# Scan ticks reordered, r operands built beside the substitution, in a two-layer decoder kernel on one Trainium2 core

## The chip, the cores and the metric

The kernel runs on one NeuronCore of a Trainium2 chip. The metric is the device time of one execution in microseconds (us), the median of several. The engines are TensorE (PE), VectorE (DVE), ScalarE (ACT), GpSimd (Pool) and SyncE (SP), which here only issues DMAs. Each has its own instruction stream, and they meet at semaphores.

## The reference

A decoder trunk of two layers, 512 tokens of width 1024, all in float32. Layer 0 is an RWKV-7 time mix (16 heads of 64) and a mixture of experts (32 experts); layer 1 is sparse attention and another mixture of experts. The change lies in the time mix:

```
r, k, v = xr @ w_r, xk @ w_k, xv @ w_v
kk = normalised(k * k_k);  k = k * (1 + (a - 1) * k_a)
step:  sa    = state @ (-kk_t)
       state = state * w_t + sa (kk_t * a_t)^T + v_t k_t^T
       y_t   = state @ r_t
y = group_norm(y) + sum(r * k * r_k) * v        # the second term is the bonus
out = (y * g) @ w_o
```

## The kernel before

**Layout.** Activations are kept transposed: eight tiles `m` of 128 channels (two heads) by 512 tokens, in regions of SBUF: `r_T`, `a_T` (from kk), `b_T` (kk * a), `k_T`, `v_T`, `g_T`, `l_T` (running log decay). The recurrence is done in chunks of 64 tokens, 8 chunks by 8 tiles = 64 packs (`PACKS`), numbered `n = 8 c + m`.

**Projections.** Weights come in tiles of 512 KB through a ring of four slots (`wring`, one region): 8 tiles each for k, v, r, and later w_o. SP loads them in the order of its program, each after the matmuls on the slot's earlier tile (`proj_mm`).

**First operands.** While PE projects v, DVE runs `k_scale(m)` (L940, L944, L945), then multiplies `a_T` by the decay (L962) and its first columns by -1 (L964, 8 elements a row), ACT makes the factor and the exponentials (L644 to L651), and Pool multiplies `b_T` (L481). PE weaves into its v matmuls, in quarters of a tile ("parts"), the product `k_inverse(m)` and, two turns later, `gram_of(m)`; DVE masks the result into `gram` (L954). SP stores the gram tiles to DRAM (L318) and, when all have landed, reads them back in another shape as `solve` (L349).

**Substitution.** The 32x32 triangular blocks are inverted column by column on DVE, steps i = 2 to 31: a product over i*i*2 elements (L976) and a reduction (L979), each waiting for the other. PE projects r beside it and ACT copies the first five r tiles out (L633). When the substitution is done SP stores the result (L354), and reads it back into `gram` with eight DMAs, four for each half of the packs (L360).

**r operands.** ACT waits for `inverse_out`. Then for each m it makes `exp(-l)` and `exp(l)` (L666, L667); DVE multiplies r * rk * k (L987) and r by the decay (L990); Pool multiplies k by the growth (L485); PE sums the first product over each head (`bonus_mm`), DVE multiplies that with v into `l_T` (`bonus_out`, L950).

**Scan.** 64 packs go through a pipeline of PE stages, one tick apart. In tick t PE runs, in this order, `rh(t-1)`, `u(t-2)`, `w(t-3)`, `u2(t-4)`, `y` and `s` of `t-5`, and last the transposes (L1569) and `p_late` products of pack t. Every stage has one PSUM bank and is copied out by ACT (`p_tr` L709, `p_rh` L678, w L685, y L702) or DVE (`p_late` L1028 and L1030, u L1004, u2 L1010, state L1018). `rh(n)` needs the copies of `p_tr` and `p_late` of pack n. Pool expands the operands of pack t+1 (L473, four products) and then, in the same tick, `x_e(t)` (L510), which needs the inverse. ACT's and DVE's orders follow PE's.

After the scan come the group norm, the w_o projection, and the rest of the network, which takes three quarters of the time.

Of the kernel before, what the change touches and what calls it, by code (L numbers as in the profile page):

```python
# [10 lines left out]
P = 128  # L11
# [3 lines left out]
NK = D // P  # L15
# [62 lines left out]
} | {f"bias_h{i}": (f"wring{i}", 128) for i in range(4)}  # L78
# [8 lines left out]
def decoder_program(nc, d, out):  # L87
    stack = ExitStack()
    with stack:
# [59 lines left out]
        tmp = region(2).rearrange("p (x s t) -> p x s t", x=4, s=2)  # L149

# [6 lines left out]
        solve = region(2)[:, 0:2048].rearrange("p (b s t) -> p b s t", b=2, s=32)  # L157
        ones_at = region(2)[:, 0:2048].rearrange("p (b n) -> p b n", b=2)[:, :, 0:1024:33]
# [129 lines left out]
        SOLVED = 1 + 2 * 30  # L288
        block = stack.enter_context(nc.Block())
# [3 lines left out]
        def _(sp):  # L293
# [16 lines left out]
            def load_ring(q, rows):  # L310
                sp.dma_start(wring[:, q % 4, :], rows).then_inc(sem(f"wring{q % 4}"), 16)
# [9 lines left out]
            for q in range(8):  # L321
# [7 lines left out]
                load_ring(q, wk_rows[q, :, :])  # L329
            for m in range(4):  # L330
                sp.wait_ge(sem("mix_used"), 24 + m + 5)
                load_ring(8 + m, d["a_wv"][m, :, :])
            sp.wait_ge(sem("mix_ready"), 48)
            sp.dma_start(head_of, d["head_of"].rearrange("h (m n) -> h m n", m=NP)).then_inc(sem("bias_in"), 16)
            for m in range(4, NP):
                sp.wait_ge(sem("proj_mm"), 8 + m - 3)
                load_ring(8 + m, d["a_wv"][m, :, :])
# [26 lines left out]
            for m in range(4):  # L364
                sp.wait_ge(sem("proj_mm"), 21 + m)
                load_ring(24 + m, wo_rows[m, :, :])
            sp.wait_ge(sem("pe_s"), PACKS)
            sp.wait_ge(sem("ev_s"), PACKS)
            for m in range(4, NP):
                sp.wait_ge(sem("wo_used"), m - 3)  # L370
                load_ring(24 + m, wo_rows[m, :, :])
# [94 lines left out]
        def _(pool):  # L466
# [1499 lines left out]
```

## Time and profile before

| | us |
|---|---|
| median of 3 runs (2197.18 to 2200.33) | 2199.89 |
| the profiled execution: time, span | 2202.11, 2200.1 |
| PE busy | 1958.9 (89%) |
| DVE, ACT, Pool busy | 705.7, 433.7, 190.6 |
| tiles for k to the start of the substitution | to 233.4 |
| substitution | 233.4 to 302.9 |
| first transposes of the scan | 330.3 |
| last tick with transposes ends | 578.3 |
| mean granted TensorE clock (share of full speed) | 0.954 |

Times within the profile are from the span's start. "Idle before" is the time an engine stood ahead of an instruction, with what released it. Granted clock is 1.00 at full speed (2.4 GHz) and 0.50 at half (1.2 GHz). PEld is the loading of weights into the array, which overlaps matmuls. A matmul of 512 float32 columns shows as two records of 0.43 us.

### The profile page before, as it was taken

Reading aid. Unit: us, or ns where it says so; the run is one execution under the profiler, and the core shown is the slowest. Engines: PE = TensorE matmul, PEld = TensorE weight load, DVE = VectorE, ACT = ScalarE, POOL = GpSimd, SP = SyncE. Lnnn points to the kernel's source line nnn. Section 1 sums busy time; section 2 is a strip of 40 time slices with the busy share of each in tenths; the row PEclk is TensorE's granted clock in tenths of the full one; section 3 lists DMA queues with packets and bytes.
Section 4 is the critical chain, followed back from the end, with each engine's and each line's share of the span. In section 5 each row is a group of like instructions: output and inputs, shape, how many; then the busy total and the mean of one; then the engine's idle time right before and its main releaser. Section 6 shows DMA issues by size and latency. Waiting matters only on the chain.

```text
span 2200.1 us, 27449 instructions
## 1 busy us (share of the span) xinstructions
PE 1958.9 (89%) x10860; PEld 1085.4 (49%) x10860; DVE 705.7 (32%) x1545; ACT 433.7 (20%) x1094; POOL 190.6 (9%) x377
## 2 busy tenths in 40 slices
PE   6999958888887999999997799999888999999993
PEld 2344417777636444444442347866546444444441
DVE  4307783444483311111110431465413111111113
ACT  2313013444401000000000201266410000000001
POOL 0002024444200000000000100011100000000001
PEclk9999977999997999999999799999997999999996
DMA  9272220000036799999995821100225999999994
GB/s 271 40 158 52 92 77 1 2 2 1 1 128 260 296 415 426 427 429 431 423 430 203 290 71 35 77 30 30 102 107 213 387 428 426 429 429 423 429 427 146
DMA packets 71750, 497.47 MB, mean 226 GB/s; under 512 B 25796, under 2 KB 30404, under 8 KB 54470
## 3 DMA queue, kind: packets, MB, share of 16 engines
q1 hardware_dynamic: 56982, 465.20, 52.0%
q10 hardware_dynamic: 12336, 22.09, 4.1%
q0 software_dynamic: 2304, 8.39, 1.1%
q8 instruction: 90, 1.47, 0.3%
q14 instruction: 38, 0.31, 0.0%
HBM read 460.46 MB, written 34.14 MB: 225 GB/s over the span
## 4 chain that ended last, share of the span: by engine, by line
PE 81%; DVE 11%; ACT 3%; issue 3%; DMA 2%; POOL 1%; ACTq 0%; SPq 0%; DVEq 0%; POOLq 0%
PE bank L1372 76%; DVE arena L976 2%; PE bank L1838 2%; ACT arena L709 1%; DVE arena L1175 1%; DVE arena L979 1%; PE bank L1569 1%; PE bank L1638 1%; DVE arena L1332 1%; PE bank L1380 1%; DMA arena<-y_rows,ints 1%; DVE arena L964 0%; DVE arena L1211 0%; DVE arena L987 0%; DMA arena<-gram 0%
## 5 line engine op out<-in xcount | busy, mean ns | idle before, releaser
L1372 PE MATMUL bank<-arena 128*64 128x512 f32 (+11 forms) x9336 | 1742.9, 425 | 66.8 <-DVE arena L1175 44.4
L1372 PEld LDWEIGHTS bank<-arena 128*128 128x128 f32 (+5 forms) x9336 | 913.6, 165 | 832.0 <-issue 724.4
L736 ACT ACTIVATE arena<-bank 128x512 f32<-128x512 f32 x64 | 38.2, 597 | 821.9 <-PE bank L1372 821.9
L1113 DVE TENSOR_TENSOR arena<-bank,vec 128x512 f32<-128x512 f32 x64 | 44.3, 692 | 346.7 <-PE bank L1372 346.7
L1167 DVE TENSOR_TENSOR arena<-arena,bank 128x256 f32<-128x256 f32 x64 | 27.0, 421 | 339.0 <-ACT arena L732 339.0
L527 POOL DMA_INDIRECT arena<-y_rows,ints x16 | 17.5, 1091 | 1233.2 <-DMA y_rows<-arena 1228.9
L473 POOL TENSOR_TENSOR arena<-arena,const 128x128 f32<-128x128 f32 x256 | 97.4, 413 | 124.3 <-PE bank L1372 123.0
L1372 PE MATMUL bank<-state,arena 128*128 128x128 f32 (+1 forms) x256 | 52.8, 337 | 42.1 <-ACT arena L709 40.2
L1372 PE MATMUL bank<-arena,const 128*128 128x512 f32 (+5 forms) x96 | 44.8, 615 | 36.8 <-DVE arena L987 21.1
L839 ACT ACTIVATE arena<-arena,small 128x128 f32<-128x128 f32 (+3 forms) x128 | 70.4, 552 | 25.2 <-DVE small L1332 25.1
L1175 DVE COPY arena<-bank 128x256 f32<-128x256 f32 x64 | 26.9, 420 | 144.6 <-PE bank L1638 144.6
L1372 PEld LDWEIGHTS bank<-state,arena 128*128 128x128 f32 x256 | 41.7, 233 | 53.4 <-ACT arena L709 51.1
L1332 DVE CUSTOM_DVE_ANT_0 arena<-bank,arena 128x128 f32<-128x128 f32 (+3 forms) x128 | 57.4, 486 | 30.9 <-PE bank L1372 30.9
L1838 PE MATMUL bank<-const,arena 128*128 128x128 f32 x320 | 48.5, 282 | 10.4 <-DVE arena L1343 10.4
L1838 PEld LDWEIGHTS bank<-const,arena 128*128 128x128 f32 x320 | 33.8, 141 | 39.1 <-issue 26.3
L551 ACT ACTIVATE arena<-arena 128x1024 f32<-128x1024 f32 x20 | 21.1, 1054 | 154.6 <-DVE arena L1061 60.5
L1372 PEld LDWEIGHTS bank<-arena,const 128*128 128x128 f32 (+1 forms) x96 | 17.5, 236 | 62.5 <-issue 28.1
L732 ACT ACTIVATE arena<-bank 128x256 f32<-128x256 f32 x64 | 24.6, 384 | 120.4 <-issue 80.4
L709 ACT ACTIVATE arena<-bank 128x384 f32<-128x384 f32 x64 | 31.4, 491 | 71.5 <-PE bank L1372 71.5
L1380 PE MATMUL bank<-const,arena 128*128 128x128 f32 x96 | 21.4, 396 | 25.4 <-DVE arena L864 25.3
L976 DVE TENSOR_TENSOR arena<-arena 128x8 f32<-128x8 f32 (+29 forms) x30 | 41.0, 1366 | 1.0
L1004 DVE COPY arena<-bank 128x128 f32<-128x128 f32 x64 | 18.7, 292 | 68.7 <-PE bank L1372 68.7
(206 smaller groups left out, 1099.3 us busy)
## 6 DMA issues: line engine op xcount, KB each, us to landing
arena<-m_w SPq DMA_DIRECT2D x64, 4096.0 KB, 21.6
arena<-m_w SPq DMA_DIRECT2D x64, 2048.0 KB, 13.5
y_rows<-arena ACTq DMA_DIRECT2D x128, 128.0 KB, 9.6
y_rows<-arena SPq DMA_DIRECT2D x2, 3840.0 KB, 41.0
arena<-kv_w SPq DMA_DIRECT2D x3, 2048.0 KB, 12.7
rev_bias<-arena ACTq DMA_DIRECT2D x1, 5120.0 KB, 56.0
arena<-a_wk SPq DMA_DIRECT2D x8, 512.0 KB, 15.6
arena<-a_wv SPq DMA_DIRECT2D x8, 512.0 KB, 3.9
```

The costliest lines, as they stand in the source:

```text
L473: nc_op = nc.gpsimd.tensor_tensor(dst.rearrange("p (a t) -> p a t", a=2), spread(src[:, m, c * C:c * C + C], 1, 2), mask, ALU.mult)
L709: nc.scalar.activation(bkv_s[:, n % 8, :], p_tr, ACT.Copy).then_inc(sem("ev_tr"), 1)
L736: nc.scalar.activation(yb[:, n % 2, :], bank[6 + n % 2][:, :], ACT.Copy).then_inc(sem("yb_ready"), 1)
L839: last = nc.scalar.activation(probs[:, n % 3, a, 0:P * (j + 1)], probs[:, n % 3, a, 0:P * (j + 1)], ACT.Exp, scale=-1.0, bias=low[:, n % 3 ...
L976: nc.vector.tensor_tensor(terms, solve[:, :, 0:i, 0:i], spread(solve[:, :, 0:i, i], 2, i), ALU.mult).then_inc(sem("solved"), 1)
L1113: nc.vector.tensor_tensor(xgT[:, p % 2, 4 * q:4 * q + 4, :], bank[2 + q][:, :].rearrange("p (k t) -> p k t", k=4), spread(v8(f"m_ln{l}")[: ...
L1167: nc.vector.tensor_tensor(gated[:, n % 2, :], silu_h[:, n % 2, :], bank[4 + n % 2][:, 256:512], ALU.mult).then_inc(sem("gated_ready"), 1)
L1175: nc.vector.tensor_copy(hT[:, n % 2, :, :, :], bank[n % 2][:, 0:256].rearrange("p (i q t) -> p i q t", i=2, q=2)).then_inc(sem("h_ready"), 1)
L1332: last = nc.vector.tensor_tensor_reduce(out=probs[:, n % 3, a, 0:P * (j + 1)], in0=bank[2 * (n % 2) + a][:, 0:P * (j + 1)], in1=bias_h[:, ...
L1372: return nc.tensor.matmul(dst, lhsT, rhs, start=start, stop=stop)
L1380: last = nc.tensor.transpose(bank[k][:, P * j:P * j + P], xn[:, j, P * k:P * k + P], ident)
L1838: last = nc.tensor.transpose(bank[4 + a][:, P * s:P * s + P], probs[:, n % 3, a, P * s:P * s + P], ident)
```

## The change

1. In the scan, PE, ACT and DVE take the transposes and their copies first in each tick, and `rh` with its copy last.
2. ACT and Pool build the r operands. ACT writes the exponentials to `r_dec` and `r_grow` (one buffer each), and copies each r tile out twice, once scaled by rk (`r_k`). Pool makes three products for each m: `r_k * k`, `r * decay`, `k * growth`. They wait for `b_ready` and `a_ready`, not for `inverse_out`. PE makes `bonus(m-1)` after r tile m. DVE takes the first five `bonus_out` between substitution steps, after steps 24, 25, 27, 29 and 30, and the rest behind.
3. `solve` moves from region 2 to slots 2 and 3 of the weight ring. v tiles 4 to 7 and all r tiles go through slots 0 and 1. v6 is loaded after store_gram(4), v7 after store_gram(7) and v5's matmuls; all r tiles after `solve`. w_o tiles wait for all r tiles.
4. The first columns of `a_T` (L964) are negated by ACT (`a_first`), which gram_of waits for.

```diff
-        solve = region(2)[:, 0:2048].rearrange("p (b s t) -> p b s t", b=2, s=32)
+        solve = region(4)[:, 2048:4096].rearrange("p (b s t) -> p b s t", b=2, s=32)
+        r_dec, r_grow = region(2)[:, 0:512], region(2)[:, 512:1024]
+        r_k = region(2)[:, 1024:2048].rearrange("p (s t) -> p s t", s=2)
+        BONUS_AT = (24, 25, 27, 29, 30)
...
# SP
-            for m in range(4, NP):
+            for m in (4, 5):
                 sp.wait_ge(sem("proj_mm"), 8 + m - 3)
-                load_ring(8 + m, d["a_wv"][m, :, :])
-            for m in range(4):
+                load_ring(m % 2, d["a_wv"][m, :, :])
+            for m in range(5):
                 store_gram(m)
             sp.wait_ge(sem("proj_mm"), 13)
-            load_ring(16, d["a_wr"][0, :, :])
-            for m in range(4, NP):
+            load_ring(0, d["a_wv"][6, :, :])
+            for m in range(5, NP):
                 store_gram(m)
             sp.wait_ge(sem("proj_mm"), 14)
-            load_ring(17, d["a_wr"][1, :, :])
+            load_ring(1, d["a_wv"][7, :, :])
             sp.wait_ge(sem("gram_out"), 32 * 16)
...
-            for m in range(2, NP):
-                sp.wait_ge(sem("proj_mm"), 13 + m)
-                load_ring(16 + m, d["a_wr"][m, :, :])
+            for m in range(NP):
+                sp.wait_ge(sem("proj_mm"), 15 + m)
+                load_ring(m % 2, d["a_wr"][m, :, :])
...
# Pool
+            pool.wait_ge(sem("a_ready"), NP)
             for m in range(NP):
                 pool.wait_ge(sem("decays"), m + 1)
+                pool.wait_ge(sem("proj_ev"), 17 + m)
+                nc.gpsimd.tensor_tensor(r_k[:, m % 2, :], r_k[:, m % 2, :], k_T[:, m, :], ALU.mult).then_inc(sem("rk_ready"), 1)
                 pool.wait_ge(sem("rk_ready"), m + 1)
-                nc.gpsimd.tensor_tensor(k_T[:, m, :], k_T[:, m, :], tmp[:, 2, m % 2, :],
-                                        ALU.mult).then_inc(sem("operands_pool"), 1)
+                nc.gpsimd.tensor_tensor(r_T[:, m, :], r_T[:, m, :], r_dec, ALU.mult).then_inc(sem("r_scaled"), 1)
+                nc.gpsimd.tensor_tensor(k_T[:, m, :], k_T[:, m, :], r_grow, ALU.mult).then_inc(sem("operands_pool"), 1)
...
# ACT
                 act.wait_ge(sem("proj_mm"), 16 + m + 1)
+                if m >= 2:
+                    act.wait_ge(sem("bonus_mm"), m - 1)
+                nc.scalar.activation(r_k[:, m % 2, :], bank[1 + (m + 2) % 3][:, :], ACT.Copy, scale=v8("rk")[:, m:m + 1])
...
+                act.wait_ge(sem("k_scaled"), m + 1)
+                nc.scalar.activation(a_T[:, m, 0::C], a_T[:, m, 0::C], ACT.Copy, scale=-1.0).then_inc(sem("a_first"), 1)
...
-            for m in range(5):
+            act.wait_ge(sem("b_ready"), NP)
+            for m in range(NP):
+                if m:
+                    act.wait_ge(sem("operands_pool"), m)
+                nc.scalar.activation(r_dec, l_T[:, m, :], ACT.Exp, scale=-DECAY)
+                nc.scalar.activation(r_grow, l_T[:, m, :], ACT.Exp, scale=DECAY).then_inc(sem("decays"), 1)
                 r_out(m)
-            act.wait_ge(sem("inverse_out"), 16)
...
# DVE
-                                               ALU.mult, ALU.mult)
-                nc.vector.tensor_scalar(kk_v[:, :, 0:1], kk_v[:, :, 0:1], -1.0, None, ALU.mult).then_inc(sem("a_ready"), 1)
+                                               ALU.mult, ALU.mult).then_inc(sem("a_ready"), 1)
...
                 nc.vector.tensor_reduce(solve[:, :, 0:i, i], terms, axis=AX.X, op=ALU.add).then_inc(sem("solved"), 1)
+                if i in BONUS_AT:
+                    bonus_out(BONUS_AT.index(i))
...
# PE
+            def bonus(m):
+                pe.wait_ge(sem("rk_ready"), m + 1)
+                if m == 0:
+                    pe.wait_ge(sem("gram_ev"), NP)
+                if m >= 2:
+                    pe.wait_ge(sem("bonus_ev"), m - 1)
+                mm(bank[6 + m % 2][:, :], head_ones, r_k[:, m % 2, :]).then_inc(sem("bonus_mm"), 1)
...
                 last.then_inc(sem("proj_mm"), 1)
+                if m:
+                    bonus(m - 1)
+            bonus(NP - 1)
...
# PE, ACT and DVE: in every tick the block of the transposes (n = tick) stands first;
# on PE and ACT the block of rh (n = tick - 1) stands last
             for tick in range(PACKS + 6):
-                n = tick - 1
-                if 0 <= n < PACKS:
+                n = tick
+                if n < PACKS:
```

## Rows read from the trace of the kernel before

**Rows 1.** Busy time by stage: window, length, engines' busy time, granted clock, DMA share, GB/s.
```profile
336.00:359.00 23.00, 19.85 (x116) 17.29 (x117) 5.95 (x23) 7.23 (x23) 9.80 (x27) 0.61 0.00 1
359.00:579.00 220.00, 184.21 (x1768) 162.91 (x1766) 89.97 (x342) 104.16 (x342) 105.57 (x279) 1.00 0.01 2
```

**Rows 2.** Chain of work in order of time: start, us, what.
```profile
336.01 1.62 PE bank L1372 x6
...
358.69 2.46 PE bank L1372 x24
...
569.80 0.33 PE bank L1569 x3
570.13 0.46 PE bank L1372 x4
570.61 0.50 ACT arena L709
...
578.93 2.93 PE bank L1372 x34
```

**Rows 3.** Timeline of one tick, PE and ACT: start, us, instruction, idle before.
```profile
571.20 0.46 PE L1372 MATMUL bank<-state,arena 128*128 128x128 f32 x2 [0.63 <-ACT arena L709]
...
571.92 0.28 ACT L678 ACTIVATE arena<-bank 128x128 f32<-128x128 f32 x1 [0.82 <-PE bank L1372]
```

**Rows 4.** Timeline around the substitution, SP's queue and DVE.
```profile
224.83 0.34 SPq L349 DMA_DIRECT2D arena<-gram  x1
...
233.40 0.11 DVE L972 MEMSET arena<- 128x64 f32 x1 [13.52 <-DMA arena<-gram]
...
302.92 0.33 SPq L354 DMA_DIRECT2D inverse<-arena  x1
306.81 5.24 SPq L360 DMA_DIRECT2D arena<-inverse  x8
```

**Rows 5.** Timeline of the first operands, DVE and Pool.
```profile
184.48 0.69 DVE L962 SCALAR_TENSOR_TENSOR arena<-arena 128x504 f32<-128x504 f32 x1
184.52 1.77 POOL L481 TENSOR_TENSOR arena<-arena 128x512 f32<-128x512 f32 x1 [172.50 <-DVE arena L945]
185.08 1.24 DVE L964 TENSOR_SCALAR arena<-arena 128x8 f32<-128x8 f32 x1
```

**Rows 6.** Timeline of the v projection's end: weight loads, PE, ACT.
```profile
203.16 0.29 PEld L1372 LDWEIGHTS bank<-arena 16*128 16x128 f32 x2 [0.76 <-issue]
...
207.22 0.29 PEld L1372 LDWEIGHTS bank<-arena 16*128 16x128 f32 x2 [0.76 <-issue]
...
218.00 1.15 PE L1372 MATMUL bank<-arena 64*64 64x64 f32 x32 [1.53 <-DVE arena L954]
...
229.68 0.60 ACT L629 ACTIVATE arena<-bank 128x512 f32<-128x512 f32 x1 [6.27 <-PE bank L1372]
```

**Rows 7.** Groups of instructions: count, busy us, mean ns, idle before.
```profile
L473 POOL TENSOR_TENSOR arena<-arena,const 128x128 f32<-128x128 f32 x256 | 97.4, 413 | 124.3 <-PE bank L1372 123.0 <-DVE arena L950 1.2
L543 POOL TENSOR_TENSOR arena<-arena 128x512 f32<-128x512 f32 x16 | 20.3, 1270 | 233.3 <-DVE arena L1359 233.3
...
L987 DVE SCALAR_TENSOR_TENSOR arena<-arena,vec 128x512 f32<-128x512 f32 x8 | 9.3, 1168 | 5.2 <-ACT arena L667 5.2
...
L950 DVE TENSOR_TENSOR arena<-bank,arena 128x512 f32<-128x512 f32 x8 | 5.5, 684 | 0.8 <-PE bank L1372 0.8
```

**Rows 8.** Timeline of the substitution: two of its 30 reductions (i = 16, 24).
```profile
246.90 0.69 DVE L979 TENSOR_REDUCE arena<-arena 128x32 f32<-128x512 f32 x1
...
268.30 1.35 DVE L979 TENSOR_REDUCE arena<-arena 128x48 f32<-128x1152 f32 x1
```

**Rows 9.** The clock: two windows (as rows 1) and PE's first work after a pause.
```profile
296.00:298.00 2.00, 0.00 (x0) 0.00 (x0) 1.97 (x2) 0.00 (x0) 0.00 (x0) 0.50 0.00 0
...
614.14 2.90 PE L1372 MATMUL bank<-arena 128*128 128x512 f32 x3 [6.39 <-issue]
...
620.00:622.00 2.00, 2.00 (x6) 0.80 (x5) 2.00 (x1) 0.00 (x0) 0.00 (x0) 0.94 0.00 0
```

More of the change, by code:

```diff
@@ L77 @@
     "cmp_w1_in0": ("router_in", 32),
-} | {f"bias_h{i}": (f"wring{i}", 128) for i in range(4)}
+} | {f"bias_h{i}": (f"wring{i}", n) for i, n in enumerate((176, 176, 80, 80))}
 def spread(ap, axis, n):
@@ L702, in _ @@
                     nc.scalar.activation(y_T[:, n % NP, (n // NP) * C:(n // NP) * C + C], p_y, ACT.Copy).then_inc(sem("ev_y"), 1)
-                n = tick
-                if n < PACKS:
-                    act.wait_ge(sem("pe_tr"), n + 1)
-                    if n >= 8:
-                        act.wait_ge(sem("pe_s"), n - 7)
-                        act.wait_ge(sem("ev_tr"), n - 7)
-                    nc.scalar.activation(bkv_s[:, n % 8, :], p_tr, ACT.Copy).then_inc(sem("ev_tr"), 1)
+                n = tick - 1
+                if 0 <= n < PACKS:
+                    act.wait_ge(sem("pe_rh"), n + 1)
+                    if n >= 2:
+                        act.wait_ge(sem("pe_u"), n - 1)
+                        act.wait_ge(sem("ev_rh"), n - 1)
+                    nc.scalar.activation(rhs_s[:, n % 2, :], p_rh, ACT.Copy).then_inc(sem("ev_rh"), 1)
             for m in range(NP):
@@ L1460, in gram_of @@
                 pe.wait_ge(sem("a_ready"), m + 1)
+                pe.wait_ge(sem("a_first"), m + 1)
                 pe.wait_ge(sem("b_ready"), m + 1)
@@ L1507, in _ @@
             for tick in range(PACKS + 6):
-                n = tick - 1
-                if 0 <= n < PACKS:
+                n = tick
+                if n < PACKS:
                     m, c = n % NP, n // NP
-                    pe.wait_ge(sem("ev_tr"), n + 1)
-                    pe.wait_ge(sem("ev_late"), n + 1)
-                    if c:
-                        pe.wait_ge(sem("ev_s"), n - NP + 1)
-                    else:
-                        pe.wait_ge(sem("state_zero"), 1)
-                    if n:
-                        pe.wait_ge(sem("ev_rh"), n)
-                    mm(p_rh, a_e[:, n % 4, :], state[:, m, :], True, False)
-                    mm(p_rh, ak_t[:, n % 4, :], bkv_s[:, n % 8, 256:384], False, True).then_inc(sem("pe_rh"), 1)
+                    pe.wait_ge(sem("ex_late"), n + 1)
+                    if n:
+                        pe.wait_ge(sem("ev_tr"), n)
+                        pe.wait_ge(sem("ev_late"), n)
+                    e = bkv_e[:, n % 2, :]
+                    cs = slice(c * C, c * C + C)
+                    for i in range(3):
+                        nc.tensor.transpose(p_tr[:, P * i:P * i + P], e[:, P * i:P * i + P], ident)
+                    mm(p_late[:, 0:64], e[:, 0:128], r_T[:, m, cs])
+                    mm(p_late[:, 64:192].rearrange("p (w t) -> p w t", w=2), e[:, 128:256],
+                       ra_T[:, :, m, cs]).then_inc(sem("pe_tr"), 1)
                 n = tick - 2
@@ L1558, in _ @@
                     mm(p_s, s8[:, 128:256], s8[:, 256:384], False, True).then_inc(sem("pe_s"), 1)
-                n = tick
-                if n < PACKS:
+                n = tick - 1
+                if 0 <= n < PACKS:
                     m, c = n % NP, n // NP
-                    pe.wait_ge(sem("ex_late"), n + 1)
-                    if n:
-                        pe.wait_ge(sem("ev_tr"), n)
-                        pe.wait_ge(sem("ev_late"), n)
-                    e = bkv_e[:, n % 2, :]
-                    cs = slice(c * C, c * C + C)
-                    for i in range(3):
-                        nc.tensor.transpose(p_tr[:, P * i:P * i + P], e[:, P * i:P * i + P], ident)
-                    mm(p_late[:, 0:64], e[:, 0:128], r_T[:, m, cs])
-                    mm(p_late[:, 64:192].rearrange("p (w t) -> p w t", w=2), e[:, 128:256],
-                       ra_T[:, :, m, cs]).then_inc(sem("pe_tr"), 1)
+                    pe.wait_ge(sem("ev_tr"), n + 1)
+                    pe.wait_ge(sem("ev_late"), n + 1)
+                    if c:
+                        pe.wait_ge(sem("ev_s"), n - NP + 1)
+                    else:
+                        pe.wait_ge(sem("state_zero"), 1)
+                    if n:
+                        pe.wait_ge(sem("ev_rh"), n)
+                    mm(p_rh, a_e[:, n % 4, :], state[:, m, :], True, False)
+                    mm(p_rh, ak_t[:, n % 4, :], bkv_s[:, n % 8, 256:384], False, True).then_inc(sem("pe_rh"), 1)
             pe.wait_ge(sem("ev_y"), PACKS)
```

96 lines of the change are left out of this document (35 added, 61 removed).

## The prediction

> **What bounds the kernel now.** I read the stages first. After the scan TensorE is busy almost without a pause to the end; nothing there is edited, and a transfer there waits only on work of that part, so I let it shift as a block. The change lies in operand building, substitution and scan. In the scan one engine should be full, yet PE is busy 184 of 220 us at full clock, after a start at an average of 0.61 [rows 1]. The chain of waits shows why [rows 2]: PE transposes pack n (0.33) and makes its `p_late` products (0.46), then stands until ACT L709 has copied `p_tr`, since `rh(n)` comes next. From 570.57 to 571.20 nothing runs on PE [rows 2, 3]. The tick is 3.864 us ((578.93 - 358.69)/57), of which 0.63 is this stall. DVE, ACT and Pool are busy 90, 104 and 106 of 220 us, under 1.9 a tick [rows 1], so PE's order is the bound.
>
> Ahead of the scan the chain is serial: gram tiles, their way through DRAM, the substitution on DVE (233.40 to 302.9), the inverse stored and read back, and only then exponentials, products, bonus and expansion [rows 4]. Tick 2 begins at 336.01 [rows 2], 33.1 us after the last reduction. Beside the substitution Pool does nothing and ACT next to nothing; PE, with the r tiles, is done before it.
>
> **Part 1: DVE's first column goes to ACT (`a_first`).** DVE L964 touches 8 elements and takes 1.24 us. It ends at 186.32, together with Pool L481 (184.52 + 1.77 = 186.29): it waits for Pool [rows 5]. Without it DVE could go 1.15 us faster in each of 8 turns, but PE then sets the pace: its turn is 4.06 us (203.16 to 207.22), and it had been standing for DVE by the end (1.53 before the gram at 218.00) [rows 6]. After the k_inverse at 207.22 the gram products start at about 208.3; two turns without k_inverse (a part of 1.72, 1.15 of gram, gaps: 3.2) put gram(7) at 214.65 instead of 218.00, so v5 ends at 219.25 instead of 222.6 (229.68 - 6.87 is its copy, 222.81) [rows 6]. The last gram store is then issued by 218.4 and lands by 220.0; the v7 load, which SP now holds until v5 is done, goes at 219.3 to 219.8. The load of `solve` leaves at 220.05, not 224.83 [rows 4]: **-4.8**. On ACT, `a_first(m)` waits for `k_scaled(m)`; v_out(2) and k_factor(m+1) queue behind it. Two exponentials and a factor (2 us) still fit before DVE's second need of them, 3 us on. Nothing charged.
>
> **Part 2: weight slots.** v6 and v7 go through two slots. v6 loads behind store_gram(4), around 210, and lands 5 us later, needed at 219.3. v7 lands about 224, needed at 226. Each r load has one tile of PE (6.87) for a landing of 3.5 to 4.7. Zero; if one is late, PE shifts by that and the slack of part 3 takes it. `solve` in other addresses: zero.
>
> **Part 3: r tiles beside the substitution.** It now starts at 220.05 + (233.40 - 224.83) = 228.6. With its own length, 69.5, and five bonus_outs of 0.68 [rows 7] placed in it (**+3.5**), it ends at 301.6 plus what the new Pool work costs it. That work is 24 products of 128x512, 1.27 each when alone [rows 7]. The before trace has no Pool product beside L976, so nearest rows bound it. When DVE L962 (both inputs in SBUF) had started 0.04 before it, Pool's L481 took 1.77; when Pool was running, L964 and L987 (1.17 on average, about 0.7 for such a shape alone, as L950) stretched to its end or past it [rows 5, 7]. L976 has both inputs in SBUF, so I let each hold the other off, and let reductions pass. A Pool product then falls into the reduction at its turn, and the next L976 starts late by 1.3 less the reduction: 0.69 long at i = 16 when r0 arrives (v6, v7 and r0, 6.87 each, after v5: 239.9), 1.35 at i = 24 [rows 8]. First tile 1.9, second 1.1, third 0.5, and about 0.9 for each of four later tiles, where a second product squeezes into the reduction; the last falls behind the final L976. **+7.0**, between 0 (they pass each other) and 17.5 (A, B and C of each tile run back to back, 3.8 less the reduction).
> The Trainium skill (SBUF — State Buffer, Who interferes with whom) says that an op with two SBUF inputs and a GpSimd op that reads SBUF exclude each other for a whole instruction, and that a reduction never contends. Rows agree for the first half (1.77 against 1.27). By it the sum below holds; without it, it would be 7 lower.
>
> Is the r chain in time? PE: r0 to 239.9, then r1, bonus0, r2, bonus1, r3 (three tiles, two products of 0.86) to 262.2; bonus2 waits for bonus_ev 1, after step 24 (36.25 into the substitution [rows 8], 264.9, and 3.5 of delays), and r4 to r7 queue behind it. Then 6.9 a tile (its copies stand 6.87 apart) plus the waits for steps 27 and 29: r7 ends about 305, ACT's copies 306, three products 310, the last bonus_out 311, expansions 0 and 1 314. The inverse is there at 308.6 + 8.3 = 316.9, so 3 us are left. PE idles 6 us before r4; in the old idle behind r7 (about 291) the clock was at the lower level by 296 [rows 9]. r4 partly at the lower level, 1.2 GHz, costs 3 us, which the waits for steps 27 and 29 take up.
>
> **Part 4: from the last reduction to tick 2.** The eight exponential and product rounds (22 us) are gone from here. What stays: store (3.9), eight inverse loads from +3.9, the first four landed at +8.3 (four issues of 0.65 and 1.9 to land) [rows 4], Pool x_e(0) 0.42, expand(2) 1.52 (four at 0.41, overlapping [rows 7]; before PE's tr(2), since x_e(0) stands ahead of it), so tick 2 at +10.35 instead of +33.1: **-22.7**.
>
> **Part 5: ticks 2 to 7.** They took 22.7 (336.01 to 358.69), at a granted clock of 0.61 on average [rows 1, 2]. In the new order PE has work without the gap from tick 2 on. Another stretch, unbroken from 614.14, had its clock back in 620 to 622 [rows 9]. With 6 us at 1.2 GHz: ticks 2 and 3 take 6.6, tick 4 (no y and s) 2.0, Pool-bound, ticks 5 and 6 3.23 each: 15.0, **-7.7**. If the clock stays low as before, ticks take twice 3.23 and it is -0.7.
>
> **Part 6: 57 full ticks.** The new first stage gives ACT a whole tick for `p_tr`. rh is now last, and u needs its copy: PE end to ACT start 0.26, copy 0.28, plus 0.06 to PE, 0.60 [rows 3], under the 0.79 of transposes and p_late [rows 2]. DVE's s copy and ACT's y copy end before their users too. 57 x 0.635: **-36.2**. At the end, with no tr to cover it, rh's copy shows once: +0.4.
>
> Sum: -4.8 + 3.5 + 7.0 - 22.7 - 7.7 - 36.2 + 0.4 = -60.5. Profiled execution 2202.11 (span 2200.1): 2141.6; it lies 2.2 above the median 2199.89, so **2139.4**; I say 2140.
>
> **Rivals.**
> - *Heavier port waits, or a late clock.* Products back to back add 10.5 (2150); the low clock to tick 7 adds 7 (2146); both 2157. For: ticks 0 and 1 come alone, with a pause before 2, and nothing shows who wins the port when both wait. Against: B waits for A's semaphore, which lets DVE in. 15% for over 2150.
> - *r chain ends last.* If PE stays at 1.2 GHz from r4 on (idle before it, waits at steps 27 and 29), a tile takes 13.7: r4 to r7 and their bonuses run from 269 to 331, the operands are ready at 337 and tick 2 comes at 342 instead of 319: 2163. For: the idle at 291 to 296 lost the clock [rows 9]. Against: r4 alone is unbroken work long enough to bring it back. 8%.
> - *The tick keeps part of its stall*, through rh's copy or expansion: at 3.5 us it adds 15, 2155. ACT is in order and rh's copy is behind y's. 6%.
> - *Slower than before.* The wait of u on rh's copy in each tick, on the path and not under the transposes. Cover is 0.79; a round trip of 1.73 (PE, ACT, PE) costs 64 x 0.94 = 60 us, all that is gained; from there on it decides. At 2.0 the time is 2140 + 64 x 1.21 = 2217. Rows give 0.60 [rows 3], but ACT is in order, and a slow y copy ahead would push it. 3%.
> - *The move buys nothing ahead of the scan*: only parts 5 and 6 remain, 2156. Needs the inverse to have been the bound already; it is not, 33.1 against 10. Inside the 6% above.
> - *Less than 2133*: no port waits at all, 2132. 5%.
>
> Likeliest, with 63%, 2133 to 2150. A difference under 0.2% (4.4 us) is about what a measurement can't tell from none. The range 2132 to 2160 leaves out the late r chain, the slow case and part of the low end, under 2 in 10. Faster 0.95, same 0.02, slower 0.03.
>
> **What would show it.** `solve` load near 220; memset near 228.6; Pool products of 1.3 to 4 us and L976 longer than before, reductions not; last reduction near 308; tick 2 near 319; granted clock 1.0 within 10 us of it; ticks of 3.23 with no PE idle. Wrong if PE waits on ACT L678's copy in each tick, if r7 is later than the inverse, or if the substitution grows by over 20.

## The result and the profile after: 2124.6 us, faster by 3.6%, below the forecast range

The changed kernel takes 2124.58 us (median of 4 runs, 2123.94 to 2126.38) against 2200.11 for the kernel before on the same chip (4 runs, 2197.18 to 2215.65): a ratio of 0.9644, 95% interval 0.9599 to 0.969. The forecast was 2140, range 2132 to 2160. The sign held, and so did the mechanism of the largest part; the gain in the profiled spans is 76.2 us (2200.1 to 2123.9) where 60.5 were forecast.

Busy time by stage in the kernel after (columns as in [rows 1]). The stages are: last reduction to tick 2, tick 2 to the start of tick 7, and the 57 full ticks (7 to 63). A tick starts with its first instruction: `rh` in the old order, the transposes in the new.

```profile
303.10:317.70 14.60, 6.26 (x21) 4.27 (x20) 2.96 (x7) 3.19 (x6) 11.06 (x21) 0.55 0.86 219
317.70:331.00 13.30, 13.30 (x116) 12.36 (x115) 5.45 (x23) 7.23 (x23) 10.78 (x29) 0.85 0.19 77
331.00:502.00 171.00, 171.00 (x1769) 158.87 (x1766) 84.59 (x343) 104.11 (x342) 104.60 (x276) 1.00 0.01 2
```

PE, the first busy column, is busy 171.00 of 171.00 us where it was 184 of 220 [rows 1], for the same 57 ticks.

SP's queue and DVE around the substitution, kernel after (as [rows 4]):

```profile
219.95 0.34 SPq L352 DMA_DIRECT2D arena<-gram  x1
...
225.98 0.11 DVE L978 MEMSET arena<- 128x64 f32 x1 [9.44 <-DMA arena<-gram]
...
303.11 0.33 SPq L357 DMA_DIRECT2D inverse<-arena  x1
307.01 5.22 SPq L363 DMA_DIRECT2D arena<-inverse  x8
```

Two ticks of PE in the kernel after (as [rows 3]; the first two lines are `rh(n-1)`, L1520 the transposes, "x14" is `p_late`, u, w and u2; the lines left out are y and s):

```profile
327.51 0.39 PE L1369 MATMUL bank<-state,arena 128*128 128x128 f32 x2
327.73 0.39 PE L1369 MATMUL bank<-arena 128*128 128x128 f32 x2
327.95 0.49 PE L1520 MATMUL bank<-const,arena 128*128 128x128 f32 x3
328.28 1.08 PE L1369 MATMUL bank<-arena 128*128 128x64 f32 x14
...
330.95 0.49 PE L1520 MATMUL bank<-const,arena 128*128 128x128 f32 x3
```

From transposes to transposes it is 3.00 us, with no idle entry. The times of both spans, split at the same events, against the terms of the forecast:

| stretch | before | after | change | forecast |
|---|---|---|---|---|
| to the substitution's start (memset) | 233.40 | 225.98 | -7.4 | -4.8 |
| substitution, to SP's store | 69.52 | 77.13 | +7.6 | +10.5 |
| store to tick 2 | 33.09 | 14.63 | -18.5 | -22.7 |
| tick 2 to the start of tick 7 | 22.68 | 13.21 | -9.5 | -7.7 |
| 57 full ticks | 220.24 | 171.00 | -49.2 | -36.2 |
| end of the scan | 10.55 | 11.63 | +1.1 | +0.4 |
| the rest of the network | 1610.6 | 1610.3 | -0.3 | 0 |
| sum | | | -76.2 | -60.5 |

The four stretches ahead of the full ticks were off by 2 to 4 us each, of both signs, together -3.1; the full ticks were off by 13.0, five sixths of the error of 15.7.

Where the chain of waits runs ahead of the scan in the kernel after (start, us, what; the first line is the third bonus product, `bonus(2)`, with r4 behind it):

```profile
266.98 9.66 PE bank L1369 x18
...
287.66 2.59 POOL arena L489
290.32 1.27 POOL arena L491
291.60 4.40 POOL arena L492
296.05 0.51 issue
296.56 0.61 ACT arena L675
...
306.99 1.27 POOL arena L489
310.41 0.70 DVE arena L957
```

The chain passes from DVE to PE at step 24 and then goes by Pool's r products and ACT's exponentials, not by the inverse.

### The profile page after: what moved, and what is told of

It is laid out like the page before. It is cut to its first block, busy times and chain, and to the rows that moved or that the text cites. A ratio compares the mean times of both kernels' runs of the same rounds, so it can differ in the third digit from the quotient of the medians.

```text
span 2123.9 us, 27456 instructions
## 1 busy us (share of the span) xinstructions
PE 1932.7 (91%) x10860; PEld 1075.2 (51%) x10860; DVE 682.8 (32%) x1521; ACT 438.3 (21%) x1110; POOL 225.5 (11%) x393
## 4 chain that ended last, share of the span: by engine, by line
PE 85%; DVE 7%; issue 3%; ACT 2%; POOL 2%; DMA 1%; ACTq 0%; DVEq 0%; SPq 0%; POOLq 0%
PE bank L1369 80%; PE bank L1840 2%; DVE arena L1172 1%; DVE arena L982 1%; PE bank L1520 1%; PE bank L1640 1%; DVE arena L1329 1%; PE bank L1377 1%; DVE arena L985 1%; DMA arena<-y_rows,ints 1%; DVE arena L1208 1%; POOL arena L489 0%; POOL arena L492 0%; DVE arena L871 0%; DMA arena<-x 0%
## 5 line engine op out<-in xcount | busy, mean ns | idle before, releaser
L1369 PE MATMUL bank<-arena,const 128*128 128x512 f32 (+5 forms) x96 | 39.9, 562 | 27.7 <-DVE arena L1091 12.2
L1369 PE MATMUL bank<-state,arena 128*128 128x128 f32 (+1 forms) x256 | 47.6, 317 | 1.9 <-DVE arena L894 1.9
L982 DVE TENSOR_TENSOR arena<-arena 128x8 f32<-128x8 f32 (+29 forms) x30 | 46.2, 1540 | 0.9
L549 POOL TENSOR_TENSOR arena<-arena 128x512 f32<-128x512 f32 x16 | 20.3, 1272 | 233.0 <-DVE arena L1356 233.0
```

The costliest lines, as they stand in the source:

```text
L982: nc.vector.tensor_tensor(terms, solve[:, :, 0:i, 0:i], spread(solve[:, :, 0:i, i], 2, i), ALU.mult).then_inc(sem("solved"), 1)
L1369: return nc.tensor.matmul(dst, lhsT, rhs, start=start, stop=stop)
```

## The experiments

Each ran beside the kernel before on its chip. A median is of 4 to 6 runs; where one run was made, it says so. The kernel before spreads more than the gains of some parts: beside experiments 1 to 3 it took 2193.18 to 2230.58 us. So their ratios are wide, and the parts are compared by their profiles, with the profile before. The landing of the solve load is given from SP's issue to DVE's memset: 8.57 us in the profile before, 6.03 in the one after.

**1. Only the new order of the scan.** The kernel before, with the stages of PE, ACT and DVE in the changed kernel's order and nothing else.

```diff
 for tick in range(PACKS + 6):
+    n = tick
+    ...   # transposes, p_late; on ACT and DVE their copies
-    n = tick - 1
-    ...   # rh
     n = tick - 2
...
-    n = tick
-    ...
+    n = tick - 1
+    ...   # PE and ACT: rh
```

> Kernel before with only the new order of the scan's stages on PE, ACT and DVE. Theory A (the stall is worth 0.86 us a tick, because the 0.63 shown is counted from a modelled end that holds the product's drain, and the weight load behind it starts late too): full ticks of 3.00 us, PE without idle time; about 2141 to 2143. Theory B (the stall is worth the 0.63 shown, and the other 0.23 comes from the rebuilt operands or the later clock): ticks of 3.23, about 2155.

Measured 2142.83 (2141.44 to 2145.34), ratio 0.9692 (0.9609 to 0.9775). A tick of its profile:

```profile
453.67 0.43 PE L1372 MATMUL bank<-arena,state 128*128 128x64 f32 x2
...
456.67 0.43 PE L1372 MATMUL bank<-arena,state 128*128 128x64 f32 x2
```

3.00 us again, with no idle between. The stall was worth 0.864 us in each tick, as theory A had it for the size, and the 3.23 of the prediction fell.

**2. Only the operands.** The changed kernel with the scan's stages in the old order (the diff above, reversed).

> Changed kernel with the old order of the scan's stages. Ticks back at 3.86 with 0.63 of idle time each. Additive theory: it keeps what the first operands and the hidden r products gave, 18 us, so about 2182; the low clock at the scan's start stays for some 20 us, as before. Rival (the two parts need each other, the earlier scan only pays with the new order): under 10 us, above 2190.

Measured 2182.99 (2182.45 to 2186.84), ratio 0.9875 (0.979 to 0.9961). The tick is 3.86 again, with the old wait:

```profile
450.41 0.46 PE L1369 MATMUL bank<-state,arena 128*128 128x128 f32 x2 [0.63 <-ACT arena L716]
...
454.27 0.46 PE L1369 MATMUL bank<-state,arena 128*128 128x128 f32 x2 [0.63 <-ACT arena L716]
```

In spans, the order alone gives 60.6 (2200.1 - 2139.5), the operands alone 19.9 (2200.1 - 2180.2), both 76.2: nearly a sum. Each alone also had a solve load that landed sooner than in the profile before (from issue to memset 5.3 and 5.9 instead of 8.6), which the sum counts twice. The low clock left sooner than expected here: it rose at about 330, 12 us after tick 2 began (318.3), and not 20.

**3. Another order without the stall.** The kernel before with y and s moved behind the transposes and `p_late`, rh still first.

```diff
     ...   # u2, tick - 4
-    n = tick - 5
-    ...   # y and s
     n = tick
     ...   # transposes and p_late
+    n = tick - 5
+    ...
```

> Kernel before with the transposes one place earlier than they were (before y and s), rh still first in the tick. Theory A (any order that keeps PE from standing gives the whole 0.86): ticks of 3.00 as in the scan-only run, within 0.05, about 2142. Rival C (the new order packs weight loads better than the old one does, apart from the stall): ticks of 3.2, about 2155. Rival D (ACT's copy of p_tr is not ready behind y and s either): idle time before rh remains, ticks above 3.3.

Measured 2150.2 (2148.75 to 2151.6), ratio 0.9722 (0.9638 to 0.9805). Its ticks take 2.955 us, and they show where the stall's size comes from. The four records of `p_late`, then y and s (128x64 x2 and x8), then rh:

```profile
452.50 0.61 PE L1372 MATMUL bank<-arena 128*128 128x64 f32 x4
452.95 0.33 PE L1372 MATMUL bank<-arena,state 128*128 128x64 f32 x2
453.12 1.11 PE L1372 MATMUL bank<-arena 128*128 128x64 f32 x8
454.06 0.39 PE L1372 MATMUL bank<-state,arena 128*128 128x128 f32 x2
454.29 0.85 PE L1372 MATMUL bank<-arena 128*128 128x128 f32 x12
```

The same four records in the kernel before, ahead of the stall:

```profile
569.96 0.61 PE L1372 MATMUL bank<-arena 128*128 128x64 f32 x4
571.20 0.46 PE L1372 MATMUL bank<-state,arena 128*128 128x128 f32 x2 [0.63 <-ACT arena L709]
571.50 0.85 PE L1372 MATMUL bank<-arena 128*128 128x128 f32 x12
```

The group is shown as 0.61 long in both. With work behind it, the next begins 0.45 after its start; ahead of the wait it is 1.24. That is 0.79, of which 0.63 stands as idle and 0.16 in the shown length of the last product. rh then takes 0.30 to its successor instead of 0.23 (0.22 in other ticks), another 0.07: together 0.86. The last 0.05 of the 0.91 that this order gains comes from how the records follow each other: the first of y is 0.06 ahead of the next instead of 0.16, the first transpose 0.16 instead of 0.11. So a little of rival C is true, 0.05 a tick. Theory A's 2142 was missed; the total is 8 us above the first experiment: its first ticks have no y and s yet to fill the gap and go on with the stall at half clock until about 353, and its solve load landed 3.2 us later.

**4. The changed kernel without the 24 Pool products.** Only a test: they are left out, so `r_T`, `k_T` and the bonus are not scaled; semaphores are raised in their place.

```diff
-                nc.gpsimd.tensor_tensor(r_k[:, m % 2, :], r_k[:, m % 2, :], k_T[:, m, :], ALU.mult).then_inc(sem("rk_ready"), 1)
-                pool.wait_ge(sem("rk_ready"), m + 1)
-                nc.gpsimd.tensor_tensor(r_T[:, m, :], r_T[:, m, :], r_dec, ALU.mult).then_inc(sem("r_scaled"), 1)
-                nc.gpsimd.tensor_tensor(k_T[:, m, :], k_T[:, m, :], r_grow, ALU.mult).then_inc(sem("operands_pool"), 1)
+                pool.sem_inc(sem("rk_ready"), 1)
+                pool.sem_inc(sem("r_scaled"), 1)
+                pool.sem_inc(sem("operands_pool"), 1)
```

> Changed kernel without the 24 products of the r operands on Pool (r_k * k, r * decay and k * growth are left out, their semaphores are still raised). Port theory: the substitution shrinks from 77.1 to about 72.5 (69.5 and five bonus_outs of 0.6), L982 at i = 21 takes 1.7 and not 2.7; tick 2 then hangs on the inverse, 10.4 behind the last reduction; about 2117. Rival (the growth is DVE waiting for PE's bonus products): the substitution stays at 77.

Measured 2114.7 (one run). The substitution takes 72.2 us (memset 224.85, store 297.02) instead of 77.1. Its step i = 21 and the end of its wait for the inverse:

```profile
248.32 1.70 DVE L981 TENSOR_TENSOR arena<-arena 128x882 f32<-128x882 f32 x1
...
304.56 0.41 POOL L515 TENSOR_TENSOR arena<-arena,const 128x128 f32<-128x128 f32 x1 [0.74 <-DMA arena<-inverse]
...
307.28 0.88 PE L1519 MATMUL bank<-const,arena 128*128 128x128 f32 x3
```

Tick 2 at 307.28 is 10.26 after the store: the +10.35 that the prediction gave for the inverse as the bound. So the products cost the substitution 5.0 us (77.13 - 72.17) and the way to tick 2 another 4.4.

**5. Who waits when DVE's and Pool's products meet.** No run of its own: the kernel after, Pool's rows first, then DVE's, at steps 21, 22 and 25 of the substitution. An instruction's shown time holds its wait for the port that the two share.

```profile
249.78 1.27 POOL L489 TENSOR_TENSOR arena<-arena 128x512 f32<-128x512 f32 x1 [2.39 <-ACT arena L642]
251.13 2.60 POOL L491 TENSOR_TENSOR arena<-arena 128x512 f32<-128x512 f32 x1
253.69 1.26 POOL L492 TENSOR_TENSOR arena<-arena 128x512 f32<-128x512 f32 x1
...
266.58 1.26 POOL L491 TENSOR_TENSOR arena<-arena 128x512 f32<-128x512 f32 x1
267.80 3.36 POOL L492 TENSOR_TENSOR arena<-arena 128x512 f32<-128x512 f32 x1
```
```profile
249.88 2.71 DVE L982 TENSOR_TENSOR arena<-arena 128x882 f32<-128x882 f32 x1
252.62 1.07 DVE L985 TENSOR_REDUCE arena<-arena 128x42 f32<-128x882 f32 x1
253.73 2.98 DVE L982 TENSOR_TENSOR arena<-arena 128x968 f32<-128x968 f32 x1
...
266.75 3.28 DVE L982 TENSOR_TENSOR arena<-arena 128x1250 f32<-128x1250 f32 x1
270.06 1.46 DVE L985 TENSOR_REDUCE arena<-arena 128x50 f32<-128x1250 f32 x1
```

DVE's product of step 21 is issued 0.10 after Pool's L489 began, and takes 2.71 where it took 1.70 without Pool's work (experiment 4). Pool's L491, issued while DVE has its turn, takes 2.60 and ends 1.14 after DVE (253.73 - 252.59). The rows of step 25 answer what the prediction left open. At 267.84 Pool's L491 ends; L492 is already issued (267.80) and DVE has been waiting since 266.75. DVE gets the turn (done at 270.03) and L492 is done 1.13 later. DVE was the one issued first. At 253.7 it was Pool, by 0.04 (253.69 against 253.73), and Pool went first: its L492 takes 1.26 and DVE's product of step 22 takes 2.98, where it takes 1.86 in experiment 4. So it is not DVE that wins but the earlier issue: of 193 pairs of overlapping products in all profiles of this study, 188 end in the order in which they were issued, and the other five were issued within 0.02 us of each other. In none of the eight tiles do two Pool products run back to back past a waiting DVE product, so a step waited for one Pool product at most, about 1.1 us. While DVE waits, its product is issued ahead of Pool's next one, and so the prediction's rival with products back to back did not come.
The Trainium skill (SBUF — State Buffer, Who interferes with whom) says that a DVE instruction with two SBUF inputs contends with a GpSimd instruction that reads SBUF, by an exclusive lock, and that a reduction never contends. This case's trace agrees: 2.71 against 1.70, and reductions of 1.07 with and without Pool. The same section says that the order of issue decides who blocks, which the 188 of 193 pairs bear out.

**6. DVE keeps the first columns.** The changed kernel with `a_first` undone.

```diff
-                                               ALU.mult, ALU.mult).then_inc(sem("a_ready"), 1)
+                                               ALU.mult, ALU.mult)
+                nc.vector.tensor_scalar(kk_v[:, :, 0:1], kk_v[:, :, 0:1], -1.0, None, ALU.mult).then_inc(sem("a_ready"), 1)
...
-                act.wait_ge(sem("k_scaled"), m + 1)
-                nc.scalar.activation(a_T[:, m, 0::C], a_T[:, m, 0::C], ACT.Copy, scale=-1.0).then_inc(sem("a_first"), 1)
...
-                pe.wait_ge(sem("a_first"), m + 1)
```

> Changed kernel with the first columns of a_T negated on DVE again. DVE's op waits for Pool's product once more (1.2 us each): the v projection ends 3.4 us later, the solve load leaves 4.8 us later. If the next weight load then falls into it again, it takes 8.4 and not 5.8: together 7.3 later, about 2132. Rival (landing not touched by that load): 4.8 later, 2129.5. Rival (the edit was hidden): no change.

Measured 2132.87 (2129.49 to 2134.5), ratio 0.9655 (0.9597 to 0.9714), 7.7 above the changed kernel run on the same chip (2125.18). The solve load is issued at 224.82, as before the change, and at 219.95 with it (219.66 in the profile on the same chip): 4.87 us, part 1's 4.8. The median fits the expected 2132, but its reason did not hold in the profile: the load took 6.77 there, not 8.4, and the two spans on this chip differ by 4.7 (2127.0 and 2122.3). What the other 3 us between the medians are stays open.

**7. Hold an r load until `solve` has landed.** The kernel before with one wait more on SP, to test whether the next weight load is what slows the solve load (8.57 against 6.03).

```diff
+            sp.wait_ge(sem("solve_in"), 16)
             for m in range(2, NP):
                 sp.wait_ge(sem("proj_mm"), 13 + m)
```

> Kernel before, with the load of r tile 2 (and all behind it) held until the solve load has landed. Theory (the 512 KB load that was issued 4.85 us into the solve load made its landing slower): the solve load takes about 5.9 us and not 8.4, the substitution starts 2.5 us earlier, about 2197.5. Rival (the landing depends on something else, so on the place of the workspace or on the store ahead of it): 8.4 us stays, no change.

Measured 2224.51 (one run). The load took 6.65. But the first experiment, with no such wait, had it in 5.34 (224.87 to 230.21), and the third in 8.59, with the same code ahead of it. The theory that the weight load sets it fell, and the cause stays open. The run showed something else, which its expectation did not have. Windows of PE in this kernel (length, busy, granted clock, DMA share, GB/s):

```profile
331.00:400.00 69.00, 61.48 (x322) 0.50 0.00 1
400.00:410.00 10.00, 9.37 (x48) 0.50 0.01 2
410.00:420.00 10.00, 8.12 (x81) 1.00 0.01 2
```

PE was busy 89% of 69 us and the clock stayed at half, 1.2 GHz, until 410. In the profile before it was back at about 354.

**8. The kernel before, once more.** Unchanged.

> The kernel before, unchanged, profiled again, for the clock at the start of its scan and the landing time of the substitution's load. Theory P (the clock's rise in the scan differs from execution to execution as long as every tick holds a pause of TensorE): the granted clock of the stretch after 332 leaves its low level anywhere between 350 and 410, and the time follows it: about 2197 if it rises at 354 as in the profile shown, up to 2225 if at 410. The load of 16 us-old columns lands in 5.2 to 8.4 us from its issue at 224.8. Theory Q (the clock's course is fixed by the code): the clock rises at 353 to 355 again, the load lands in 8.4 and the time is 2200 within 3.

Measured 2207.27 (one run). The clock rose at about 358, 24 us after tick 2 began (333.84), and the solve load took 6.39 (224.80 to 231.19). So both differ between executions of one code, which is theory P; but the time did not follow the rise as P had it (2197 for 354), so that number of it was wrong. The scan's last stall ends at 579.53, 0.6 later than in the profile before, since the load's 2.2 us went to the later clock; the rest of the difference lies behind that point, 1625.8 us to the end of the span against 1621.2, and no run says why.

**9. First bonus output two steps earlier.** The changed kernel, where PE had stood 4.63 us at 266.98 for `bonus_ev`, queued behind step 24.

```diff
-        BONUS_AT = (24, 25, 27, 29, 30)
+        BONUS_AT = (22, 25, 27, 29, 30)
```

> The changed kernel, with one number of BONUS_AT altered: the first of the five bonus outputs stands after step 22 of the substitution instead of 24. In the changed kernel TensorE reached the second bonus product at 266.98 after 4.63 us without work, because it waits there for VectorE's first bonus output after step 24; the fourth projection product (r4) then ran at the low clock for 7.81 us. Theory P (the wait for that output is what stops TensorE, and nothing on the critical path follows from it): the idle time before that product shrinks to about 1 us, TensorE's work on r4 keeps its clock, the substitution keeps its length of 77.1 us within 0.5, and the time is that of the changed kernel within 2 us. Rival Q (the late projection is what makes GpSimd's products collide with the substitution): the products start 3 to 5 us earlier, the port waits shift to other steps, the last GpSimd product ends 3 us earlier than 310.81 and the time falls by 3 us.

Measured 2120.6 (2120.13 to 2121.83), ratio 0.962 (0.9561 to 0.9679). The product that waited is `bonus(2)`, the third, ahead of r4. Here it runs without a wait:

```profile
261.02 1.02 PE L1369 MATMUL bank<-arena,const 128*128 128x512 f32 x2
261.88 7.03 PE L1369 MATMUL bank<-arena 128*128 128x512 f32 x16
```
and in the changed kernel:

```profile
266.98 2.04 PE L1369 MATMUL bank<-arena,const 128*128 128x512 f32 x2 [4.63 <-DVE arena L957]
268.81 7.81 PE L1369 MATMUL bank<-arena 128*128 128x512 f32 x16
```

The bonus product takes 1.02 instead of 2.04 and r4 7.03 instead of 7.81. PE does not finish sooner by it: it now waits 0.87, 2.19 and 2.79 us at the next three bonus products, r7 takes 8.73 and ends at 300.35, against 299.80 in the changed kernel. What comes sooner is r4, and with it Pool's products on it, at 272.30 instead of 277.98, and Pool had been the pace from there on. Theory P's "time as before" fell and rival Q was right in direction: Pool's last product ends at 305.5 and not at 310.81. The substitution is 78.4 long instead of 77.1, which P had within 0.5, and tick 2 comes 9.43 after the store.

Since that ran on another chip than the changed kernel, both were run side by side.

> The changed kernel, unchanged, as the partner of the next kernel on the same chip. Both theories: 2124 to 2126, tick 2 about 14.6 us after SP's store, the last Pool product about 7.7 after it.

> The first bonus output after step 22 instead of 24, beside the changed kernel on one chip. Theory P (TensorE's wait for that output makes the r chain the last ahead of the scan): tick 2 comes 9.5 to 10.5 us after SP's store instead of 14.6, and the median lies 3 to 5 us under its partner's, with most runs apart. Rival Q (the 4 us seen before came from another chip or from the landing of the substitution's load): the medians agree within 1.5 us.

Measured 2127.77 for the changed kernel (6 runs, 2125.17 to 2129.18; ratio 0.9595, 0.9543 to 0.9647) and 2124.45 with the earlier output (6 runs, 2122.21 to 2126.09; ratio 0.958, 0.9529 to 0.9632): 3.3 us, theory P. (The changed kernel was expected at 2124 to 2126 and lay 1.8 above.) The profile of the second, its store, Pool's last product and expansion, and PE's transposes of tick 2:

```profile
303.81 0.33 SPq L357 DMA_DIRECT2D inverse<-arena  x1
```
```profile
304.03 1.26 POOL L492 TENSOR_TENSOR arena<-arena 128x512 f32<-128x512 f32 x1
...
311.58 0.41 POOL L516 TENSOR_TENSOR arena<-arena,const 128x128 f32<-128x128 f32 x1 [0.98 <-DMA arena<-inverse]
```
```profile
314.06 0.87 PE L1520 MATMUL bank<-const,arena 128*128 128x128 f32 x3
```

Tick 2 is 10.25 after the store, and what `x_e(0)` waits for is the inverse again. Beside it the changed kernel has 14.63 (304.00 to 318.63). So the wait for the first bonus output is what made the r chain last, shown by taking it away in two profiles; this is the best version found.

**10. Two buffers for the exponentials.** The changed kernel, where Pool stands 2.39 us in six of the eight tiles while ACT refills the one `r_dec` and `r_grow` and copies the r tile out. The state tile, which lends the second pair, is zeroed after the first expansion instead.

```diff
-        r_dec, r_grow = region(2)[:, 0:512], region(2)[:, 512:1024]
+        spare = state[:, :, :].rearrange("p m n -> p (m n)")
+        r_dec = [region(2)[:, 0:512], spare[:, 0:512]]
+        r_grow = [region(2)[:, 512:1024], spare[:, 512:1024]]
...
-                if m:
-                    act.wait_ge(sem("operands_pool"), m)
+                if m >= 2:
+                    act.wait_ge(sem("operands_pool"), m - 1)
```

> The changed kernel with a second pair of buffers for the decay exponentials that GpSimd's r products read (in the state tile, which is zeroed after the first expansion instead of ahead of the products). Theory P (the chain of ScalarE's exponentials and GpSimd's products, with 2.39 us of GpSimd idle per column tile while ScalarE refills the single buffer, is what ends last ahead of the scan): the last product ends at least 3 us earlier than 310.81, the first transposes start about 3.5 us earlier, up to the limit that the reload of the inverse sets (10.3 us from the last reduction to tick 2 instead of 14.6), and the last output projection starts 3 to 4 us earlier than 513.58. What of this reaches the end depends on the clock behind the scan: if it does not fall there, the time is 2121; if it falls in the scan's last ticks as it did with both edits together, where the first 20 output products took 11.50 us instead of 8.82, the time is 2124. Rival Q (the products collide with the substitution more when they are closer together): the substitution grows by 2 to 4 us beyond 77.1 and nothing is won.

Measured 2124.39 (2121.53 to 2129.11), ratio 0.964 (0.958 to 0.9701): no difference in the median from the changed kernel, which did not run on this chip. In its profile Pool's last product ends at 305.2 and the first output product starts at 508.58 instead of 513.58, somewhat more than theory P had. The clock did not fall there, for which P had 2121; the profiled execution took 2123.07 (span 2120.4). The runs spread over 7.6 us; a gain shows in that profile (3.5 us of span) and not in the median.

**11. Both edits together.** The changed kernel with the diffs of 9 and 10. The changed kernel itself was run again on that chip.

> The changed kernel once more, beside the version above on one chip: 2124.6 as before, within 2 us.

> Changed kernel with the first bonus_out after step 22 and not 24, and two buffers each for r_dec and r_grow (the second pair in the state tile, zeroed behind). Theory (in the changed kernel the r chain, not the inverse, released the first ticks): Pool's last product ends about 6 us earlier, tick 2 starts 10.3 behind the last reduction and not 14.6, about 2120.5. Rival (Pool's products, closer together, hold DVE's products off more): the last reduction comes 3 or 4 us later and nothing is won, 2124.

Measured 2124.75 with both (2120.59 to 2126.3, 6 runs), ratio 0.9611 (0.9566 to 0.9655), and 2125.18 for the changed kernel (2124.24 to 2130.15, 6 runs), ratio 0.9625 (0.958 to 0.967). The theory's 2120.5 fell, and the rival's 2124 fits by its number alone: the substitution grew by 0.8 (77.93) and not by 3 to 4, and tick 2 came 10.6 after the store. The profiled execution reaches the output projection at 510.10, 3.48 earlier than the changed kernel, yet its span is 2123.6 against 2123.9. In it:

```profile
508.09 1.48 PE L1372 MATMUL bank<-arena 128*128 128x64 f32 x8
510.10 11.50 PE L1372 MATMUL bank<-arena,const 128*128 128x512 f32 x20 [0.54 <-DVE state L1030]
```
and the same product groups in the changed kernel:

```profile
511.94 1.11 PE L1369 MATMUL bank<-arena 128*128 128x64 f32 x8
513.58 8.82 PE L1369 MATMUL bank<-arena,const 128*128 128x512 f32 x20 [0.54 <-DVE state L1027]
```

11.50 against 8.82: in this execution the granted clock fell to half at about 509, in the last ticks, where PE waits 0.29 to 0.54 for DVE each time, and 2.7 of the 3.5 us were gone. The changed kernel has the same waits and kept its clock there, so nothing here says what decides. The side-by-side run of experiment 9 shows it too (510.10, 11.57). An earlier arrival can be given back this way, and it was not in the profiles that arrived at 507.95, 508.58 and 513.61. The rest behind this point is no constant either: 1609.5 to 1612.5 us in the profiles of changed kernels in which the clock stayed, so gains of 3 us need medians side by side.

## Why the prediction was wrong, step by step

**Part 6, the full ticks (-36.2 forecast, -49.2 measured): the step that failed.** The mechanism held: the wait for `p_tr`'s copy goes, and u's wait for rh's copy is covered in all 57 ticks. The size was wrong. "57 x 0.635" took the stall from the idle entry. The price of a wait is the distance of two starts with it less the same distance without it: 1.24 - 0.45 around the wait, and 0.07 more for rh, 0.86. That the stall was worth this is shown by experiments 1 and 3, which get 0.86 and 0.91 by two orders without touching anything else. The Trainium skill (Perfetto Trace Analysis, Tensor Engine Instruction) says that the end of a TensorE record is an estimate of the profiler and not an observation; the trace agrees, since the same four products carry 0.61 where their successor starts after 0.45.

**Part 4, tick 2 (-22.7, measured -18.5).** +10.35 after the store was right for the inverse (10.26 in experiment 4), but in the changed kernel the inverse wasn't last. Part 3 had asked whether the r chain is in time and paced it by PE, "6.9 a tile". Pool got r4 late, behind PE's wait for the first bonus output (278.0; 272.3 in experiment 9), and from there on the pace was Pool's: three products (3.8), 2.39 in which ACT makes the next exponentials into the single buffers and copies r out, and up to 4.5 of waits for the port: 9.7, 10.7 and 8.6 us a tile at the end. The last bonus output ended at 311.1, where the prediction had it (311), but by luck: PE was faster than forecast and Pool slower. But its 3 us of slack were counted against an inverse at 316.9, and the substitution, forecast to end at 308.6, ended at 303.1: with the inverse 5.5 us earlier, the r chain was last. PE was done with r7 at 299.8 instead of 305, and Pool's pace took those 5 us. The rival "r chain ends last" is what happened, by another cause than the one given (the clock of PE) and at 4.3 us instead of 23.

**Part 3, the substitution (+10.5, measured +7.6).** Five bonus outputs cost 0.48 each, 2.4 instead of 3.5: from a reduction's start to the next product's start it is 1.87 at step 24 where it is 1.39 without the output. Port waits cost the other 5.2 instead of 7.0, within 0 to 17.5; the experiment without Pool's products gives 5.0. The open question, who goes first when both wait, goes to the one issued first.

**Part 1 (-4.8, measured -7.4).** The solve load was issued at 219.95 against 220.05 forecast; experiment 6 confirms 4.9 for the edit. The other 2.5 is the landing, 6.03 instead of 8.57. Over all profiles of this study it was 5.3 to 8.6, and no run says by what, so this share of the miss was chance as far as is known.

**Part 5 (-7.7, measured -9.5).** The clock was back at 322, 4 us after tick 2 and not 6, and the last of these ticks take 3.00 as well. **The tail (+0.4, measured +1.1):** in ticks 64 and 65 nothing covers the round trip to ACT, 0.37 of idle shown each. **Part 2 (0):** no r tile was late by its weights. No other rival came in; the time fell under 2133, but by the ticks and with the port waits present, not without them as the rival "less than 2133" had it.

## What to carry to other kernels

Price a stall of TensorE by starts, not by the idle entry: from the start of the group ahead of the wait to the start behind it, less the same distance in a stretch without the wait. The same holds for an instruction put into a chain on VectorE: the bonus output is shown at 0.68, and costs 0.48. In a pipeline of stages, put enough other work between the stage whose result goes out to another engine and its reader: more than a whole tick in experiment 1, y and s in experiment 3; the two orders gained 0.86 and 0.91 us a tick. When work is moved beside a long serial stage, pace it by the slowest of its engines with its buffers counted (here one buffer, 2.39 us a tile), and look at which wait stops the feeder: one number, 24 to 22, was worth 3.3 us. Ask then what stands behind the feeder: TensorE was done no sooner, only r4 was.

## What the runs showed of the hardware that was not expected

- The clock at the start of the scan. With a pause of 0.63 in each tick it stayed at 1.2 GHz after tick 2 began for 12 us (experiment 2), 18 (kernel before), 24 (experiment 8), and in another execution till 410, with PE busy 89% (experiment 7). With no pause it was back 1 to 4 us after tick 2 in the profile after and in those of the same order that were read for it (experiments 1, 6, 9, 10, 11). Nothing in the runs says what decides between the first four. It may also be why, on the chip of the side-by-side run, the kernel before spreads from 2198.22 to 2229.96 us with mean clocks from 0.957 to 0.941, while the changed one stays within 2125.17 to 2129.18: time and clock go together, but the cause is argued only.
- DVE and Pool waiting for the shared port: at the end of a Pool product DVE got its turn, although the next Pool product had been issued, because DVE's had been issued before it (266.75 against 267.80). A Pool product that had waited ended 1.13 to 1.14 us after DVE's, less than its own 1.27.
- The 1024 KB read that starts the substitution took 5.3 to 8.6 us to the memset for the same code.
